# RG-LRU gate products from operands split into high and low parts, on TensorE

## The chip, the cores and the metric

One core of one Trainium2 chip. The metric is the device time of one execution of the whole kernel in microseconds (us). Every operand starts in device memory and the output ends there. The profile is of one execution; its times count from the start of the span, which runs from the first to the last recorded instruction.

## The reference

A trunk of two layers on x (1 x 512 x 1024, float32): one recurrent layer, one differential-attention layer that reads one shared K/V, each followed by a squared-ReLU MLP of width 4096. The change lies in the recurrent layer alone:

```
xy = rmsnorm(x) @ w_in + b_in            # 1024 -> 2048
xb, yb = split(xy);  gate = gelu(yb)
xc = causal_conv4(xb, conv_w) + conv_b   # per channel
g = einsum('bsnc,gncd->gbsnd', xc in 8 blocks of 128, gate_w) + gate_b
r = sigmoid(g[0]);  i = sigmoid(g[1])
log_a = -8 * r * softplus(-lam);  a = exp(log_a)
bx = sqrt(-expm1(2 * log_a)) * (i * xc)
hs = scan(h_t = a_t * h_(t-1) + bx_t)
out = (hs * gate) @ w_out
```

The gates' products are block-diagonal: for each of 8 blocks of 128 channels two products of a 128x128 weight with 128 x 512 values.

## The kernel before

Channels lie on the 128 partitions, the 512 positions in the free dimension; a chunk m is one block of 128 channels. Each engine runs a queue of its own in an order written out by hand, and counting semaphores join them: `wait_ge` holds an engine's queue until a semaphore has a value, so everything behind the waiting instruction waits too.

The large products are computed in three passes. A weight tile of 128 x 1024 (eight 128x128 blocks) is loaded by SP into `w_raw` (two buffers), ScalarE copies it to `w_hi` in the type float32r (`split_hi`, L630), VectorE subtracts to give `w_lo` (`split_lo`, L1167), and TensorE adds up w_hi x hi, w_hi x lo and w_lo x hi over the eight chunks: 24 matmuls of 128x128 by 128x512 (L1916). `w_hi` and `w_lo` have four slots, and a tile's PSUM bank is one of four, so tile t needs bank t-4 read. The load of tile r is issued when `split_lo` of tile r-2 is done; `split_hi(t)` waits for the load and for tile t-4 on TensorE.

The input product has 16 tiles, in the order x0 x1 x2 x3 x4 y0 x5 y1 x6 y2 x7 y3 y4 y5 y6 y7. VectorE evicts an x tile into `pad` (`branch`, L1289) and a y tile into `gelu` (`y_scaled`, L1295), scaled by `rstd`, which `norm_guess` on ScalarE and `norm_newton` on VectorE make just before the first eviction. For each chunk then: `tap` (ScalarE, L713) and `conv` (VectorE, three steps, L1301) give the convolution in `lru_v`; `gates(m)` (TensorE, L1975) makes the two gate products in two PSUM banks; `sigmoids` (ScalarE, L720 and L722), `gated_input` (VectorE, L1312), `tanh` (L729), `decay_exp` (L734), `decayed` (VectorE, L1318 and L1322), `root` (ScalarE, L739 and L741), `scaled_input` (L1328), `recurrence` (a scan, L1334), `gelu_of` (L746), `gated` (L1340), `gated_hi` (L751) and `gated_lo` (L1345) lead to the split operand of the output product. That starts with three tiles opened side by side, chunk by chunk (`open_tiles`), each step waiting for its chunk's `gated_lo`. Chunk m's gates stand in TensorE's queue behind input tile 4 (chunk 0), 5 (1 and 2), 6 (3), 7 (4), 9 (5), 10 (6) and 12 (7).

In `gates(m)` the weights `gw` and the moving operand `lru_v[:, m, :]` are plain float32, unsplit. `gw` is loaded by a DMA in ScalarE's queue (L699). ScalarE's functions belong to table sets; an ACT_TABLE_LOAD stands ahead of a function that the loaded set lacks (sigmoid and tanh share one, exp, sqrt and gelu need others; Copy and Identity never bring one).

Of the kernel before, what the change touches and what calls it, by code (L numbers as in the profile page):

```python
# [8 lines left out]
P = 128  # L9
D = 1024  # L10
S = 512
NCH = D // P
# [7 lines left out]
TILE = NCH * P  # L20
# [165 lines left out]
def build(nc, x_t, weights, gate_weights, vectors, lam_vecs, final_gain, out):  # L186
    F32 = mybir.dt.float32
# [5 lines left out]
    with keep:  # L193
        def sb(name, shape, dt, stack=keep):
            return stack.enter_context(nc.sbuf_tensor(name, shape, dt))

        def sem(name):
            return keep.enter_context(nc.semaphore(name))
# [11 lines left out]
        lru_v = sb("lru_v", [P, NCH, S], F32, region)  # L210
        lru_x = sb("lru_x", [P, NCH, S], F32, region)
        gelu = sb("gelu", [P, NCH, S], F32, region)
        sb("between", [P, 2, S], F32, region)
        early = ExitStack()
        gw = sb("gw", [P, 2 * NCH * P], F32, early)
        pad = sb("pad", [P, NCH, PAD + S], F32, early)
        early.close()
        out_hi = sb("out_hi", [P, NCH, S], F32R, region)
        out_lo = sb("out_lo", [P, NCH, S], F32R, region)
        region.close()  # L220
# [39 lines left out]
        results.close()  # L260
        prob = sb("prob", [P, 2, 2, S], F32)
        prob_t = sb("prob_t", [P, 2, S], F32)
        work = sb("work", [P, 4, S], F32)
        r21 = work[:, 0:2, :].rearrange("p n s -> p (n s)")
        a_sum = work[:, 2:4, :].rearrange("p n s -> p (n s)")
# [63 lines left out]
        conv_consts = sem("conv_consts")  # L329
        tap_done = sem("tap_done")  # L330
        conv_done = sem("conv_done")
        gates_mm = sem("gates_mm")
        gates_act = sem("gates_act")
        ix_done = sem("ix_done")
# [275 lines left out]
        def _(act):  # L610
            own = Own(act, act_own)
            def split_hi(t):
                if t >= TILES:
                    return
                quarter = quarter_of(t)
                if quarter is None:
                    r = RING_OF[t]
                    act.wait_ge(raw_in[r % RAWS], 16 * (r // RAWS))
                    src = w_raw[:, r % RAWS, :]
                else:  # L620
                    layer, g, (q, loaded, sums, adds), half = quarter
                    act.wait_ge(quarter_in[q][half], quarter_loads(layer, g, loaded))
                    if sums:
                        act.wait_ge(sum_in[q][half], quarter_sums(layer, g, q, sums))
                    if adds:
                        act.wait_ge(quarter_added, quarter_adds(layer, g, adds - 1, half))
                    src = QUARTERS[q][:, half, :]
                if t >= RING:
                    act.wait_ge(tile_done, t - RING + 1)
                nc.scalar.activation(w_hi[:, t % RING, :], src, ACT.Copy).then_inc(whi_done, 1)  # L630
# [26 lines left out]
            def norm_guess(n):  # L657

                act.wait_ge(stats_done, n + 1)
                k = n + (n > N_KV)  # L660
                by_cols, by_rows = cols[:, 1, :], work[:, 3, :]
                if n != N_A:
                    take_log(by_cols, ps[:, BANK_COLS, 0:QB], k)
                if n in (N_A, N_KV):
                    take_log(by_rows, ps[:, BANK_STATS, :], k + (n == N_KV))
                if n != N_A:
                    take_root(by_cols, k)
                if n in (N_A, N_KV):
                    take_root(by_rows, k + (n == N_KV))
# [40 lines left out]
            def tap(m):  # L710

                act.wait_ge(bank_read, XT[m] + 1)
                nc.scalar.activation(lru_v[:, m, :], pad[:, m, PAD:], ACT.Identity,  # L713
                                     scale=col("conv_w", PAD * NCH + m),
                                     bias=conv_c[:, m:m + 1]).then_inc(tap_done, 1)

            def sigmoids(m):
                act.wait_ge(gates_mm, m + 1)
                bank_r, bank_i = BANK_GATES[m % 2]
                nc.scalar.activation(lru_r[:, m, :], ps[:, bank_r, :], ACT.Sigmoid,  # L720
                                     bias=col("gate_b", m))
                nc.scalar.activation(lru_x[:, m, :], ps[:, bank_i, :], ACT.Sigmoid,  # L722
                                     bias=col("gate_b", NCH + m)).then_inc(gates_act, 1)

            def tanh(m):

                act.wait_ge(gates_act, m + 1)
                act.wait_ge(ix_done, m + 1)
                nc.scalar.activation(lru_v[:, m, :], lru_r[:, m, :], ACT.Tanh,  # L729
                                     scale=small[:, 8, m:m + 1]).then_inc(tanh_done, 1)  # L730

            def decay_exp(m):
                act.wait_ge(tanh_done, m + 1)
                nc.scalar.activation(lru_r[:, m, :], lru_r[:, m, :], ACT.Exp,  # L734
                                     scale=small[:, 9, m:m + 1]).then_inc(lru_exp, 1)

            def root(m):
                act.wait_ge(lru_q, m + 1)
                nc.scalar.activation(lru_v[:, m, :], lru_v[:, m, :], ACT.Sqrt,  # L739
                                     scale=-1.0).then_inc(sqrt_done, 1)  # L740
                nc.scalar.activation(lru_r[:, m, :], lru_r[:, m, :], ACT.Copy, scale=-1.0,  # L741
                                     bias=1.0).then_inc(lru_a, 1)
# [10 lines left out]
            act.wait_ge(consts_done, 1)  # L753
            split_hi(4)
            split_hi(5)
            norm_guess(N_A)
            act.wait_ge(conv_consts, 1)
            act.wait_ge(decay_done, 3)
            split_hi(6)
            tap(0)  # L760
            tap(1)
            tap(2)
            split_hi(7)
            split_hi(8)
            sigmoids(0)
            tap(3)
            tanh(0)
            tap(4)
            split_hi(9)
            sigmoids(1)  # L770
            sigmoids(2)
# [2 lines left out]
            tanh(2)  # L774
            split_hi(10)
            sigmoids(3)
            decay_exp(1)
            tap(5)
            decay_exp(2)
# [1 line left out]
            root(0)  # L781
            root(1)
            root(2)
            sigmoids(4)
            tanh(3)
            split_hi(12)
# [1 line left out]
            tanh(4)  # L788
            decay_exp(3)
            decay_exp(4)  # L790
            sigmoids(5)
            split_hi(13)
            split_hi(14)
# [1 line left out]
            sigmoids(6)  # L795
            tap(7)
            decay_exp(5)
            root(3)
            root(4)
            root(5)  # L800
# [353 lines left out]
        def _(dve):  # L1154
# [131 lines left out]
            def branch(m):  # L1286
                t = XT[m]
                dve.wait_ge(tile_done, t + 1)
                nc.vector.tensor_tensor(pad[:, m, PAD:], ps[:, t % RING, :], rstd[:, :],  # L1289
                                        ALU.mult).then_inc(bank_read, 1)  # L1290
# [7 lines left out]
            def conv(m):  # L1298
                dve.wait_ge(tap_done, m + 1)
                for j in range(PAD - 1, -1, -1):  # L1300
# [6 lines left out]
                    else:  # L1307
                        ins.then_inc(conv_done, 1)

            def gated_input(m):  # L1310
                dve.wait_ge(gates_act, m + 1)
                nc.vector.tensor_tensor(lru_x[:, m, :], lru_x[:, m, :], lru_v[:, m, :],  # L1312
                                        ALU.mult).then_inc(ix_done, 1)
# [12 lines left out]
            def scaled_input(c):  # L1326
                dve.wait_ge(sqrt_done, c + 1)
                own.step(nc.vector.tensor_tensor(lru_x[:, c, :], lru_x[:, c, :], lru_v[:, c, :],  # L1328
                                                 ALU.mult))
# [17 lines left out]

            split_lo(4)
            decay()
            norm_newton(N_A)  # L1350
            dve.wait_ge(conv_consts, 1)
            split_lo(5)
            branch(0)
# [2 lines left out]
            branch(2)  # L1356
            conv(0)
            branch(3)
            conv(1)
            split_lo(7)  # L1360
            branch(4)
            gated_input(0)
            conv(2)
            conv(3)
            gated_input(1)
            split_lo(8)
            y_scaled(0)
            gated_input(2)
            conv(4)
            branch(5)  # L1370
            split_lo(9)
            decayed(0)
            split_lo(10)
# [3 lines left out]
            y_scaled(1)  # L1377
            conv(5)
            scaled_input(0)
            recurrence(0)  # L1380
            split_lo(11)
            branch(6)
# [3 lines left out]
            split_lo(12)  # L1386
            conv(6)
            y_scaled(2)
            scaled_input(2)
            decayed(3)  # L1390
            gated_input(5)
# [3 lines left out]
            recurrence(2)  # L1395
            conv(7)
            decayed(5)
            gated_input(6)
            split_lo(14)
            y_scaled(3)  # L1400
# [508 lines left out]
        def _(pe):  # L1909
# [52 lines left out]
                ins.then_inc(stats_done, 1)  # L1962

            def gates(m):
                pe.wait_ge(conv_done, m + 1)
                if m == 0:
                    pe.wait_ge(gw_in, 16)
                if m == 1:

                    pe.wait_ge(rstd_done, N_A + 1)  # L1970
                if m >= 2:
                    pe.wait_ge(gates_act, m - 1)
                for g, bank in enumerate(BANK_GATES[m % 2]):
                    ws = slice((g * NCH + m) * P, (g * NCH + m + 1) * P)
                    ins = nc.tensor.matmul(ps[:, bank, :], gw[:, ws], lru_v[:, m, :], start=True, stop=True)  # L1975
                ins.then_inc(gates_mm, 1)

            pe.wait_ge(consts_done, 1)
# [424 lines left out]
```

## Time and profile before

| what | value |
|---|---|
| median of 3 runs | 1041.56 us (1040.28 to 1042.02) |
| the profiled execution | 1041.43 us |
| its span | 1038.9 us |
| mean granted TensorE clock | 0.997 |
| TensorE (PE) busy | 1022.2 us, 98% |
| VectorE (DVE) busy | 821.1 us, 79% |
| ScalarE (ACT) busy | 652.5 us, 63% |
| the 32 records of the gate products | between 37.4 and 95 us |

PE is TensorE's matmuls, PEld its weight loads, DVE VectorE, ACT ScalarE, POOL GpSimd, SP the queue that issues most loads. A float32 matmul shows as two records of the same instruction. A matmul's record is longer than the step from one start to the next, since matmuls are pipelined.

### The profile page before, as it was taken

How to read it: one execution, taken by the hardware profiler on the slowest of the kernel's cores; microseconds unless marked ns; L12 is line 12 of the kernel's file. 1: busy time of each engine (PE TensorE's matmuls, PEld its weight loads, DVE VectorE, ACT ScalarE, POOL GpSimd, SP SyncE). 2: the span in 40 equal slices, each digit the busy share in tenths (PEclk: the TensorE clock that was granted, in tenths of full speed). 3: DMA queues.
4: the chain of work that ended last, by engine and by line, in shares of the span. 5: the costliest groups of instructions: out<-in, count | busy, mean ns of one | idle time of the engine just before them, and what ended most of it. 6: DMA issues, size and time to landing. Idle time of an engine off the chain costs nothing.

```text
span 1038.9 us, 15457 instructions
## 1 busy us (share of the span) xinstructions
PE 1022.2 (98%) x5984; PEld 887.6 (85%) x5984; DVE 821.1 (79%) x1173; ACT 652.5 (63%) x956; POOL 107.7 (10%) x133
## 2 busy tenths in 40 slices
PE   8999999999999999999999999999999999999995
PEld 5777889989979989988888888879989989989984
DVE  7998886896896896898756877768697697697696
ACT  7698776745745755755436676757764664664665
POOL 1000110121111111010000000011021011011012
PEclk9999999999999999999999999999999999999998
DMA  7222856498498498472422111286498589589672
GB/s 254 87 92 65 227 142 185 114 255 231 113 244 239 118 241 242 121 182 82 122 61 62 62 62 62 89 229 131 160 206 222 180 198 231 179 185 229 194 171 93
DMA packets 47592, 165.29 MB, mean 159 GB/s; under 512 B 5408, under 2 KB 5536, under 8 KB 47392
## 3 DMA queue, kind: packets, MB, share of 16 engines
q1 hardware_dynamic: 31536, 109.59, 30.7%
q0 software_dynamic: 15552, 53.48, 28.5%
q10 hardware_dynamic: 432, 1.24, 0.3%
q8 instruction: 47, 0.77, 0.3%
q14 instruction: 25, 0.20, 0.1%
HBM read 159.05 MB, written 2.10 MB: 155 GB/s over the span
## 4 chain that ended last, share of the span: by engine, by line
PE 83%; DVE 7%; DMA 4%; issue 3%; ACT 2%; POOL 0%; SPq 0%; DVEq 0%; ACTq 0%; POOLq 0%
PE ps L2049 27%; PE ps L2084 24%; PE ps L1916 21%; PE ps L2147 4%; DVE w_lo L1167 3%; DMA w_raw<-weights 2%; PE ps L2211 2%; PE ps L2236 2%; PE ps L1975 1%; DMA q<-weights 1%; ACT w_hi L630 1%; PE ps L2225 1%; DVE r L1508 1%; DVE value L1546 1%; DMA x<-x_t 1%
## 5 line engine op out<-in xcount | busy, mean ns | idle before, releaser
L2049 PE MATMUL ps<-x_hi,w_hi 128*128 128x256 f32 x896 | 254.0, 284 | 0.2 <-DVE x_lo L1448 0.2
L2049 PE MATMUL ps<-x_hi,w_lo 128*128 128x256 f32 x896 | 253.6, 283 | 0.0
L2049 PE MATMUL ps<-x_lo,w_hi 128*128 128x256 f32 x896 | 253.5, 283 | 0.0
L630 ACT ACTIVATE w_hi<-w_raw 128x1024 fp32r<-128x1024 f32 x134 | 140.1, 1052 | 142.9 <-DMA w_raw<-weights 105.5
L1167 DVE TENSOR_TENSOR w_lo<-w_raw,w_hi 128x1024 fp32r<-128x1024 f32 x134 | 164.0, 1224 | 74.7 <-ACT w_hi L630 74.0
L1167 DVE TENSOR_TENSOR w_lo<-q,w_hi 128x1024 fp32r<-128x1024 f32 x144 | 176.5, 1229 | 48.6 <-ACT w_hi L630 47.8
L630 ACT ACTIVATE w_hi<-q 128x1024 fp32r<-128x1024 f32 x144 | 151.0, 1052 | 96.6 <-PE ps L2049 44.4
L2084 PE MATMUL ps<-w_hi,a_hi 128*128 128x512 f32 x448 | 176.3, 393 | 2.0 <-DVE w_lo L1167 1.2
L2084 PE MATMUL ps<-w_hi,a_lo 128*128 128x512 f32 x448 | 174.7, 390 | 0.0
L2084 PE MATMUL ps<-w_lo,a_hi 128*128 128x512 f32 x448 | 174.6, 390 | 0.0
L2049 PEld LDWEIGHTS ps<-x_hi,w_hi 128*128 128x128 f32 x896 | 171.9, 192 | 0.7 <-DVE x_lo L1448 0.4
L2049 PEld LDWEIGHTS ps<-x_lo,w_hi 128*128 128x128 f32 x896 | 172.0, 192 | 0.3
L2049 PEld LDWEIGHTS ps<-x_hi,w_lo 128*128 128x128 f32 x896 | 172.0, 192 | 0.0
L559 POOL DMA_DIRECT2D q<-weights x96 | 82.5, 941 | 836.3 <-DMA q<-weights 473.1
L2084 PEld LDWEIGHTS ps<-w_hi,a_hi 128*128 128x128 f32 x448 | 84.1, 188 | 26.0 <-issue 5.3
L2084 PEld LDWEIGHTS ps<-w_lo,a_hi 128*128 128x128 f32 x448 | 84.1, 188 | 17.8
L2084 PEld LDWEIGHTS ps<-w_hi,a_lo 128*128 128x128 f32 x448 | 84.2, 188 | 16.4
L1546 DVE SCALAR_TENSOR_TENSOR value<-ps,scale,value 128x512 f32<-128x512 f32 x104 | 73.1, 744 | 3.0 <-PE ps L2084 2.6
L1916 PE MATMUL ps<-in_hi,w_hi 128*128 128x512 f32 x128 | 53.6, 419 | 2.8 <-DVE in_lo L1172 1.4
L1916 PE MATMUL ps<-in_hi,w_lo 128*128 128x512 f32 x128 | 49.9, 390 | 0.0
L1916 PE MATMUL ps<-in_lo,w_hi 128*128 128x512 f32 x128 | 49.9, 390 | 0.0
L1535 DVE TENSOR_TENSOR a_lo<-work,a_hi 128x1024 fp32r<-128x1024 f32 x32 | 39.0, 1220 | 0.0
(226 smaller groups left out, 1670.3 us busy)
## 6 DMA issues: line engine op xcount, KB each, us to landing
w_raw<-weights SPq DMA_DIRECT2D x134, 512.0 KB, 4.2
q<-weights POOLq DMA_DIRECT2D x96, 512.0 KB, 7.9
q<-weights SPq DMA_DIRECT2D x64, 512.0 KB, 4.7
x<-x_t SPq DMA_DIRECT2D x8, 256.0 KB, 6.2
y_t<-value SPq DMA_DIRECT2D x8, 256.0 KB, 2.3
acc<-work POOLq DMA_DIRECT2D x6, 256.0 KB, 3.5
rstd<-work POOLq DMA_DIRECT2D x6, 256.0 KB, 3.3
w_raw<-weights SPq DMA_DIRECT2D x4, 256.0 KB, 4.6
```

The source lines that it names most:

```text
L559: nc.gpsimd.dma_start(QUARTERS[q][:, half, :], weights[stored_tile(layer, g, place + half)], accum_op=ALU.add).then_inc(sum_in[q][half], 16)
L630: nc.scalar.activation(w_hi[:, t % RING, :], src, ACT.Copy).then_inc(whi_done, 1)
L1167: nc.vector.tensor_tensor(w_lo[:, t % RING, :], src, w_hi[:, t % RING, :], ALU.subtract).then_inc(wlo_done, 1)
L1508: nc.vector.tensor_tensor(to[:, :], to[:, :], banks, ALU.add).then_inc(up_added, 1)
L1535: nc.vector.tensor_tensor(a_lo[:, k % SLOTS, :, :].rearrange("p n s -> p (n s)"), src, a_hi[:, k % SLOTS, :, :].rearrange("p n s -> p (n s)"),
L1546: return nc.vector.scalar_tensor_tensor(out=to, in0=bank, scalar=scale2[:, half, tok:tok + 1], in1=to, op0=ALU.mult, op1=ALU.add)
L1916: ins = nc.tensor.matmul(ps[:, bank, :], w[:, slot, ws], o[:, k, :], start=(k == 0 and n == 0), stop=(k == NCH - 1 and n == 2))
L2049: ins = nc.tensor.matmul(to, w[:, t % RING, ws], o[:, op, j, :], start=fresh and j == 0 and f % 2 == 0 and n == 0, stop=j == PAIRS - 1 and ...
L2084: ins = nc.tensor.matmul(ps[:, bank, :], a[:, a_slot, j, ts], w[:, slot, ws], start=first and a is a_hi and w is w_hi, stop=end and w is w ...
L2147: ins = nc.tensor.matmul(ps[:, 4 * half + tok, :], o[:, k, ts], w[:, t % RING, cs], start=(i == 0 and n == 0), stop=(i == NCH - 1 and n == 2))
L2211: ins = nc.tensor.matmul(ps[:, BANK_SCORES + 2 * (j % 2) + c, 0:n], q[rows, :], k[rows, :], start=i == 0, stop=i == 2)
L2236: ins = nc.tensor.matmul(ps[:, BANK_O, qb * P:(qb + 1) * P], prob_t[:, j % 2, kb * P:(kb + 1) * P], value[:, kb, h * P:(h + 1) * P], start ...
```

## The change

`gw` is split once into `gw_hi` (ScalarE, a float32r copy in two instructions of 128 x 1024) and `gw_lo` (VectorE, a subtract in two instructions, written over `gw`). For each chunk `conv_hi` (ScalarE) copies the convolution's result to `xc_hi` as float32r and `conv_lo` (VectorE) subtracts to give `xc_lo`; both have two buffers, so `conv_hi(m)` also waits for the products of chunk m-2. `gates(m)` makes six float32r matmuls of 128x128 by 128x512 in place of two float32 ones, and waits for `conv_lo(m)` in place of `conv(m)`. `between`, an unused spacer, moves behind the early tensors; `xc_hi` and `xc_lo` lie over `work`.

```diff
+            def gate_weights_hi(n):
+                ks = slice(n * TILE, (n + 1) * TILE)
+                act.wait_ge(gw_in, 16)
+                nc.scalar.activation(gw_hi[:, ks], gw[:, ks], ACT.Copy).then_inc(gw_hi_done, 1)
+            def conv_hi(m):
+                act.wait_ge(conv_done, m + 1)
+                if m >= 2:
+                    act.wait_ge(gates_mm, m - 1)
+                nc.scalar.activation(xc_hi[:, m % 2, :], lru_v[:, m, :], ACT.Copy).then_inc(xc_hi_done, 1)
...
+            def gate_weights_lo(n):
+                ks = slice(n * TILE, (n + 1) * TILE)
+                dve.wait_ge(gw_hi_done, n + 1)
+                nc.vector.tensor_tensor(gw_lo[:, ks], gw[:, ks], gw_hi[:, ks], ALU.subtract).then_inc(gw_lo_done, 1)
+            def conv_lo(m):
+                dve.wait_ge(xc_hi_done, m + 1)
+                nc.vector.tensor_tensor(xc_lo[:, m % 2, :], lru_v[:, m, :], xc_hi[:, m % 2, :],
+                                        ALU.subtract).then_inc(xc_lo_done, 1)
...
             def gates(m):
-                pe.wait_ge(conv_done, m + 1)
+                pe.wait_ge(xc_lo_done, m + 1)
                 if m == 0:
-                    pe.wait_ge(gw_in, 16)
+                    pe.wait_ge(gw_lo_done, 2)
...
-                    ins = nc.tensor.matmul(ps[:, bank, :], gw[:, ws], lru_v[:, m, :], start=True, stop=True)
+                    for i, (w, o) in enumerate(((gw_hi, xc_hi), (gw_hi, xc_lo), (gw_lo, xc_hi))):
+                        ins = nc.tensor.matmul(ps[:, bank, :], w[:, ws], o[:, m % 2, :], start=i == 0, stop=i == 2)
```

The queues of the changed kernel up to the last chunk, with what is added in capitals:

- ScalarE: split_hi(4), split_hi(5), GATE_WEIGHTS_HI(0), norm_guess, GATE_WEIGHTS_HI(1), split_hi(6), tap(0), tap(1), tap(2), CONV_HI(0), split_hi(7), CONV_HI(1), split_hi(8), sigmoids(0), tap(3), tanh(0), CONV_HI(2), tap(4), CONV_HI(3), split_hi(9), sigmoids(1), sigmoids(2), tanh(1), decay_exp(0), tanh(2), split_hi(10), sigmoids(3), CONV_HI(4), decay_exp(1), tap(5), decay_exp(2), split_hi(11), root(0), root(1), root(2), CONV_HI(5), sigmoids(4), tanh(3), split_hi(12), tap(6), tanh(4), decay_exp(3), decay_exp(4), CONV_HI(6), sigmoids(5), split_hi(13), split_hi(14), tanh(5), sigmoids(6), tap(7), decay_exp(5), CONV_HI(7), root(3), ...
- VectorE: split_lo(4), decay, GATE_WEIGHTS_LO(0), norm_newton, GATE_WEIGHTS_LO(1), split_lo(5), branch(0), split_lo(6), branch(1), branch(2), conv(0), branch(3), CONV_LO(0), conv(1), split_lo(7), CONV_LO(1), branch(4), gated_input(0), conv(2), conv(3), CONV_LO(2), CONV_LO(3), gated_input(1), split_lo(8), y_scaled(0), gated_input(2), conv(4), branch(5), CONV_LO(4), split_lo(9), decayed(0), split_lo(10), gated_input(3), decayed(1), decayed(2), y_scaled(1), conv(5), scaled_input(0), CONV_LO(5), recurrence(0), split_lo(11), branch(6), scaled_input(1), recurrence(1), gated_input(4), split_lo(12), conv(6), y_scaled(2), CONV_LO(6), scaled_input(2), decayed(3), gated_input(5), branch(7), decayed(4), split_lo(13), recurrence(2), conv(7), decayed(5), CONV_LO(7), gated_input(6), ...

## Rows read from the trace of the kernel before

**Rows 1.** The page, busy time, share of the span and instructions.
```profile
PE 1022.2 (98%) x5984; PEld 887.6 (85%) x5984; DVE 821.1 (79%) x1173; ACT 652.5 (63%) x956; POOL 107.7 (10%) x133
```

**Rows 2.** The chain that ended last: start us, us, what.
```profile
29.85 1.23 DVE w_lo L1167
...
31.82 5.72 PE ps L1916 x24
37.55 1.72 PE ps L1975 x4
...
95.06 59.89 PE ps L1916 x264
```

**Rows 3.** TensorE's waits, 28 to 125 us: in total, times, longest.
```profile
PE ps L1916 <- DVE pad L1289: 0.4, 1, 0.4
```

**Rows 4.** TensorE's time line: start us, us, line, instruction, idle time before.
```profile
1.65 3.78 PE L1981 MATMUL ps<-three_halves,ones 128*128 128x512 f32 x4 [1.65 <-POOL cols L520]
...
37.16 0.39 PE L1916 MATMUL ps<-in_hi,w_lo 128*128 128x512 f32 x1
37.39 1.88 PE L1975 MATMUL ps<-lru_v,gw 128*128 128x512 f32 x4
...
39.33 0.40 PE L1916 MATMUL ps<-in_lo,w_hi 128*128 128x512 f32 x1
...
1029.09 0.39 PE L2084 MATMUL ps<-w_lo,a_hi 128*128 128x512 f32 x1
```

**Rows 5.** VectorE's time line, the same columns.
```profile
29.85 1.23 DVE L1167 TENSOR_TENSOR w_lo<-w_raw,w_hi 128x1024 fp32r<-128x1024 f32 x1
30.99 0.68 DVE L1289 TENSOR_TENSOR pad<-ps,rstd 128x512 f32<-128x512 f32 x1
...
33.92 2.32 DVE L1301 SCALAR_TENSOR_TENSOR lru_v<-pad,vec,lru_v 128x512 f32<-128x512 f32 x3
36.16 0.68 DVE L1289 TENSOR_TENSOR pad<-ps,rstd 128x512 f32<-128x512 f32 x1
...
55.42 0.69 DVE L1318 SCALAR_TENSOR_TENSOR lru_r<-lru_r,lru_v 128x512 f32<-128x512 f32 x1
...
56.75 1.22 DVE L1167 TENSOR_TENSOR w_lo<-w_raw,w_hi 128x1024 fp32r<-128x1024 f32 x1
...
65.73 1.22 DVE L1334 TENSOR_TENSOR_SCAN lru_v<-lru_r,lru_x 128x512 f32<-128x512 f32 x1
```

**Rows 6.** ScalarE's time line, the same columns.
```profile
38.72 1.28 ACT L720 ACT_TABLE_LOAD   x1
40.01 0.69 ACT L720 ACTIVATE lru_r<-ps,vec 128x512 f32<-128x512 f32 x1
40.60 0.68 ACT L722 ACTIVATE lru_x<-ps,vec 128x512 f32<-128x512 f32 x1
41.17 0.81 ACT L713 ACTIVATE lru_v<-pad,conv_c,vec 128x512 f32<-128x512 f32 x1
...
97.69 1.06 ACT L630 ACTIVATE w_hi<-w_raw 128x1024 fp32r<-128x1024 f32 x1
...
103.64 0.73 ACT L734 ACTIVATE lru_r<-lru_r,small 128x512 f32<-128x512 f32 x1
104.27 0.62 ACT L751 ACTIVATE out_hi<-lru_v 128x512 fp32r<-128x512 f32 x1
```

**Rows 7.** The ring's loads issued between 30 and 60 us.
```profile
DMA to landing us min/median/max: 3.3/3.5/4.4
```

**Rows 8.** The gate weights' load, its issue (first and last start).
```profile
L699 ACTq DMA_DIRECT2D gw<-gate_weights x1: 335/335/335, 12.8 to 12.8; - x1
```

**Rows 9.** A window near the end: busy by engine, granted clock, DMA share, GB/s.
```profile
1033.00:1033.50 0.50, 0.00 (x0) 0.00 (x0) 0.02 (x1) 0.45 (x1) 0.00 (x0) 0.67 0.50 188
```

**Rows 10.** VectorE's waits, 30 to 125 us: in total, times, longest.
```profile
DVE pad L1289 <- PE ps L1916: 3.3, 2, 2.7
DVE lru_x L1312 <- ACT lru_x L722: 2.0, 3, 1.3
...
```

More of the change, by code:

```diff
@@ L212, in build @@
         gelu = sb("gelu", [P, NCH, S], F32, region)
-        sb("between", [P, 2, S], F32, region)
+        early = ExitStack()
+        gw_lo = sb("gw_lo", [P, 2 * NCH * P], F32R, early)
+        early.close()
         early = ExitStack()
         gw = sb("gw", [P, 2 * NCH * P], F32, early)
+        gw_hi = sb("gw_hi", [P, 2 * NCH * P], F32R, early)
         pad = sb("pad", [P, NCH, PAD + S], F32, early)
         early.close()
+        sb("between", [P, 2, S], F32, region)
         out_hi = sb("out_hi", [P, NCH, S], F32R, region)
@@ L262, in build @@
         prob_t = sb("prob_t", [P, 2, S], F32)
+        early = ExitStack()
+        xc_hi = sb("xc_hi", [P, 2, S], F32R, early)
+        xc_lo = sb("xc_lo", [P, 2, S], F32R, early)
+        early.close()
         work = sb("work", [P, 4, S], F32)
@@ L331, in build @@
         conv_done = sem("conv_done")
+        gw_hi_done = sem("gw_hi_done")
+        gw_lo_done = sem("gw_lo_done")
+        xc_hi_done = sem("xc_hi_done")
+        xc_lo_done = sem("xc_lo_done")
         gates_mm = sem("gates_mm")
@@ L755, in _ @@
             split_hi(5)
+            gate_weights_hi(0)
             norm_guess(N_A)
+            gate_weights_hi(1)
             act.wait_ge(conv_consts, 1)
@@ L762, in _ @@
             tap(2)
+            conv_hi(0)
             split_hi(7)
+            conv_hi(1)
             split_hi(8)
@@ L767, in _ @@
             tanh(0)
+            conv_hi(2)
             tap(4)
+            conv_hi(3)
             split_hi(9)
@@ L776, in _ @@
             sigmoids(3)
+            conv_hi(4)
             decay_exp(1)
@@ L783, in _ @@
             root(2)
+            conv_hi(5)
             sigmoids(4)
@@ L790, in _ @@
             decay_exp(4)
+            conv_hi(6)
             sigmoids(5)
@@ L797, in _ @@
             decay_exp(5)
+            conv_hi(7)
             root(3)
@@ L1349, in _ @@
             decay()
+            gate_weights_lo(0)
             norm_newton(N_A)
+            gate_weights_lo(1)
             dve.wait_ge(conv_consts, 1)
@@ L1358, in _ @@
             branch(3)
+            conv_lo(0)
             conv(1)
             split_lo(7)
+            conv_lo(1)
             branch(4)
@@ L1364, in _ @@
             conv(3)
+            conv_lo(2)
+            conv_lo(3)
             gated_input(1)
@@ L1370, in _ @@
             branch(5)
+            conv_lo(4)
             split_lo(9)
@@ L1379, in _ @@
             scaled_input(0)
+            conv_lo(5)
             recurrence(0)
@@ L1388, in _ @@
             y_scaled(2)
+            conv_lo(6)
             scaled_input(2)
@@ L1397, in _ @@
             decayed(5)
+            conv_lo(7)
             gated_input(6)
```

## The prediction

> **What bounds the kernel now.** I read the page first: TensorE is busy for 98% of the span [rows 1]. Then the chain that ended last: from 95.06 us it runs 59.89 us through TensorE alone, and around the gates it is TensorE too, tile of weights by tile of weights, with 1.72 us for each pair of gate products [rows 2]. Just ahead of that it is VectorE's: a w_lo subtract at 29.85, then the first eviction, and TensorE's tile 4 starts at 31.82 [rows 2], 0.4 us late, the only wait TensorE has between 28 and 125 us [rows 3]. So what TensorE loses or saves in this stage arrives at the end unchanged, and what VectorE is given before 31.8 is paid in full. Elsewhere in the stage VectorE and ScalarE work for nearly all of the time, in hand-written orders, and the question is whether their new work still comes before TensorE asks for it. My working is the trace's time line carried on, queue by queue.
>
> **TensorE's saving.** A gate pair is two unsplit 128x512 products, shown as four records. The last tile matmul starts at 37.16, the second one after the pair at 39.33; less two ordinary steps of 0.227 (the steps ahead of 37.39 in the row; a tile of 24 takes 5.45) the pair costs 2.17 - 0.45 = 1.72 us [rows 4]. The new six products have the shape and types of the tile's own: 6 x 0.227 = 1.36 us. Eight pairs save 8 x 0.36 = 2.9 us. Each restart after a wait costs 0.08 (0.31 instead of 0.23), the only dearer bound.
> The page "FP8 and Floating Point Precision", section TensorE Precision Notes, of the Trainium skill says that a true FP32 product takes four passes through the array. By that the pair would be eight passes against six, a quarter saved, 0.43 us of 1.72 and 3.4 us over the eight; the trace's six single steps leave less, and the sum goes by the trace.
>
> **Prices on the two feeders.** Instructions that wait for nothing start 0.08 to 0.1 us before the end of the one ahead (w_lo 29.85 + 1.23, next at 30.99 [rows 5]), so each counts with its duration less 0.09. VectorE: 1.14 for a 1024-wide subtract or a scan, 0.60 for a 512-wide one, 2.24 for a convolution, 1.33 for decayed() [rows 5]. ScalarE: 0.97 for 1024 wide, 0.52 for a 512-wide Copy, 0.59 and 0.58 for the sigmoids, 0.7 for a tap, 0.63 for tanh or exp, and 1.28 for each table load, which starts as soon as the queue reaches it, even before its operand is there [rows 6]. The in-place subtract gw_lo over gw has no twin in this stage; I price it as the row of its shape. A ring load is issued when w_lo two tiles earlier is done, and lands 3.5 us later (3.3 to 4.4) [rows 7]. gw itself is issued at 12.8 [rows 8], ten us before it is now first read, so its load costs nothing. The added ScalarE and VectorE work is 2 x 0.97 + 8 x 0.52 = 6.1 us and 2 x 1.14 + 8 x 0.60 = 7.1 us.
>
> **Before tile 4.** gate_weights_hi(0) and (1) sit in ScalarE's idle time and end at 25.3 and 27.6, hidden. gate_weights_lo(0), after decay(), and gate_weights_lo(1), before split_lo(5), are both on the chain to branch(0): 2 x 1.14 = 2.28 us. branch(0) ends at 33.95, tile 4 starts at 34.10 in place of 31.82. **+2.28.**
>
> **gates(0).** conv(0) ends at 38.52 (36.24 + 2.28). conv_hi(0) ends 39.17, conv_lo(0) 39.89, so gates(0) can start at 40.04; tile 4 gives TensorE free at 39.67. **+0.45** with the restart. It ends at 41.5, and tile 5 fills TensorE to 46.9.
>
> **gates(2), the large one.** VectorE goes on with conv(1) 39.80 to 42.12. ScalarE has conv_hi(1) queued behind that wait: 42.16 to 42.78. Behind it stand split_hi(8) (to 43.7), and only then the table load for sigmoids(0) (43.74 to 45.02) and the two sigmoids, to 46.30; before, they were done at 41.28 [rows 6]. VectorE's gated_input(0) waits for them, until 46.33, and behind it are conv(2), from 46.93 to 49.25, and conv(3), to 51.49. conv_lo(2) stands behind conv(3): 51.40 to 52.09. TensorE, after gates(1) (46.93 to 48.29), needs xc_lo(2) and gets it at 52.24. Before, it ran gates 1 and 2 without a gap. **+3.95 + 0.08.** gates(1) itself is covered (conv_lo(1) ends 43.87). After gates(2) TensorE stands at 53.7, 5.7 us later than before.
>
> **What is late next.** conv_hi(3) waits for conv(3) and ends at 52.15; split_hi(9), sigmoids(1) and (2) follow to 55.45; gated_input(1) is let go at 54.3; split_lo(8) ends only at 56.14 and so the load of tile 10 lands at 59.9. ScalarE's split_hi(10) waits for it (TensorE frees the ring slot at 59.4 anyway), then come a table load, sigmoids(3) and conv_hi(4), 63.46 to 64.08. VectorE is through with branch(5) at 60.09 and stands in conv_lo(4) for 4.0 us, to 64.12; the result is there at 64.81, before TensorE ends tile 7 at 65.94: gates(3) and (4) cost no wait. But split_lo(9) now ends at 65.94, the load of tile 11 lands at 69.7 and holds ScalarE at split_hi(11); roots 0 to 2 run to 75.3, conv_hi(5) to 75.9, conv_lo(5) to 76.6, against gates(5) asked for at 78.2: covered by 1.5 us. Then ScalarE: sigmoids(4) to 78.5, tanh(3), split_hi(12), tap(6) to 80.8. VectorE: recurrence(0), split_lo(11), branch(6), scaled_input(1), recurrence(1), gated_input(4), split_lo(12) from 76.5 to 83.1, conv(6) to 85.39, y_scaled(2). conv_hi(6) ends at 86.05, conv_lo(6) at 86.77, and TensorE has finished tile 10 at 85.01: gates(6) at 86.92. **+1.91 + 0.08.** gates(7) is asked for at 99.3 and its operand is ready at 97.7: covered.
>
> **The output product.** TensorE reaches the three open tiles at 117.0 (before 111.3). Each step of three k chunks lasts 2.04. ScalarE and VectorE are later by about 8.5 us than before there: gated_lo(0) ends at 115.1, in time; gated_lo(1) stands behind split_lo(18), which waits for gelu(3), gelu(4) and split_hi(18), and ends at 119.57, while TensorE asks at 118.33: **+1.39.** Behind it chunks 2 to 7 come 0.1 to 3 us before they are asked for (the last at 131.2, asked for at 132.0). Everything behind lies as before, shifted: TensorE is the chain again.
>
> **Sum.** 2.28 + 0.45 + 4.03 + 1.99 + 1.39 - 2.9 = +7.2 us. The profiled execution took 1041.43 us (span 1038.9 and 2.5 around it), the median of the runs is 1041.56; I take 1041.4 + 7.2 = **1048.6 us**. The least certain terms are the last two, 3.4 us together, since they are differences of long queues: a table load or a DMA of 1 us more or less moves them fully. 0.2% of the time, 2.1 us, is about what can be told from no change.
>
> **Rivals.**
> The late stalls don't come. VectorE has 4 us of idle time in my line at conv_lo(4), and if ScalarE's queue is 2 us faster than I make it, gates(6) and the output product are covered. Then 2.28 + 0.45 + 4.03 - 2.9 = +3.9: 1045.3 us. Against it: both engines' waits in my line come from a load and a ring slot, which no faster arithmetic moves.
> The clock falls in the wait at gates(2). Before, the granted clock was still 1.00 until 1033.0 and 0.67 in the next half microsecond, on the way to 0.50 [rows 9], 3.7 us after the last matmul, started at 1029.09, had ended [rows 4]; my wait is 3.8 to 3.9 us, at the edge. At the low clock the four warm-up records took 3.78 us where the four gate records take 1.88 [rows 4], and at 6.36 the pace was full: 1.9 to 2.4 us lost. As gates(6) is held by VectorE and not by TensorE, up to 2.0 of it is swallowed there: 1048.6 to 1049.0; if the wait at gates(6) isn't there for other reasons, or gates(2) comes later still, up to 1051. The page "TensorE: Matmul & The Clock Gate" of the Trainium skill, section HAM oscillation, has the rule that a pause in TensorE's work halves its clock and each restart then begins slowly; the fall at 1033 agrees.
> It comes out faster, or the same. If ScalarE reached sigmoids(0) before conv_hi(1)'s wait mattered, or conv_lo(2) were ready by 48.3, the one stall of 4.03 would be gone and with it the later two, and 2.28 + 0.45 - 2.9 = -0.2 remains: 1041.2. To be faster by 2.1 us, the 2.28 ahead of tile 4 must be hidden too, -2.9: 1038.5. It decides at stalls of 2.9 us in all. Against it: the order of VectorE alone (conv(2), conv(3), conv_lo(2) behind gated_input(0)) puts 5.8 us between the end of sigmoids(0) and xc_lo(2), while TensorE has one tile and one pair.
> Two engines' added work might also cost its whole 7.1 us on top of my waits, were there no idle time to take it up; VectorE waited for 9.0 us between 30 and 125, the sum of six rows of which the two largest are shown [rows 10], and could take it up; so I give that little, 1052 us and more.
>
> **Chances.** My line, with its neighbours 1046.3 to 1050: 0.62. Late stalls gone, 1044 to 1046.3: 0.15. Clock or further waits, 1050 and over: 0.13. Stalls absent, no change: 0.05; faster by over 0.2%: 0.05. The range 1044 to 1051.8 leaves out these last two and some 5 in 100 above. Faster 0.05, same 0.05, slower 0.90.
>
> **What would show it.** In the profile of the changed kernel: TensorE waiting 2.3 us more ahead of tile 4, for the pad eviction; six matmuls of 0.39 at a step of 0.23 in place of four of 0.59; a wait of about 4 us for xc_lo near 48 us, the largest of the stage; another of about 2 us near 85; one of over 1 us for out_lo near 118; VectorE idle for 4 us near 60, let go by xc_hi; sigmoids(0) ending near 46.3. The forecast falls if xc_lo(2) is ready by 48, which needs sigmoids(0) some 4 us sooner, or if TensorE later waits for something now hidden from it, so that the delay is taken up there.

## The result, and the profile after

The changed kernel takes 1051.22 us in the median (1051.01 to 1052.82, 4 runs), the kernel before 1040.92 on the same occasion: a ratio of 1.0103, 95% interval 1.0091 to 1.0115. It is 10.3 us slower. The forecast was 1048.6, slower by 7.2, with a range of 1044.0 to 1051.8: the direction and the range held, the difference was 3.1 us larger than forecast. Two later sets of executions of the same two kernels put it at 9.5 and 8.9 us, so it is 1.7 to 3.1 us above the forecast's 7.2. The profiled execution of the changed kernel took 1051.01 us; its span is 1048.5 and its mean granted clock 0.992.

TensorE's waits of the changed kernel, 28 to 125 us, the same view as [rows 3]:

```profile
PE ps L2031 <- DVE xc_lo L1352: 3.4, 2, 2.6
PE ps L1971 <- DVE pad L1324: 2.1, 1, 2.1
PE ps L1971 <- DVE out_lo L1390: 1.2, 1, 1.2
```

Where there was one wait of 0.4 us there are four, and they are the ones that were named: ahead of tile 4, twice for xc_lo, once for out_lo. TensorE's time line shows where, and what the passes cost now (compare [rows 4]):

```profile
33.35 0.47 PE L1971 MATMUL ps<-in_hi,w_hi 128*128 128x512 f32 x1 [2.07 <-DVE pad L1324]
...
51.45 0.50 PE L2031 MATMUL ps<-xc_hi,gw_hi 128*128 128x512 f32 x1 [2.61 <-DVE xc_lo L1352]
...
66.80 0.39 PE L2031 MATMUL ps<-xc_hi,gw_hi 128*128 128x512 f32 x1
67.03 0.39 PE L2031 MATMUL ps<-xc_lo,gw_hi 128*128 128x512 f32 x1
...
68.16 0.39 PE L1971 MATMUL ps<-in_hi,w_hi 128*128 128x512 f32 x1
...
86.80 0.50 PE L2031 MATMUL ps<-xc_hi,gw_hi 128*128 128x512 f32 x1 [0.80 <-DVE xc_lo L1352]
...
119.55 0.50 PE L1971 MATMUL ps<-out_hi,w_hi 128*128 128x512 f32 x1 [1.18 <-DVE out_lo L1390]
```

Six passes from 66.80 to 68.16 are 1.36 us, to the digit. The bracket is idle time counted from the modelled end of the record ahead, 0.16 us (0.39 less a step of 0.23) after TensorE could have issued the next; so 2.07 there is 2.23 by the prediction's way of counting.

The stage's end is best read from one line, VectorE's eviction of the output product, which is the same instruction in both kernels. Durations min/median/max, then first and last start; before, and after:

```profile
L1455 DVE TENSOR_TENSOR x<-x,ps x8: 678/680/689, 125.8 to 155.0; 128x512 f32<-128x512 f32 x8
```

```profile
L1510 DVE TENSOR_TENSOR x<-x,ps x8: 679/680/689, 132.8 to 162.1; 128x512 f32<-128x512 f32 x8
```

The last start moves from 155.0 to 162.1: 7.1 us in the stage, where 7.2 were forecast. The span grew by 9.6. So 2.5 us of this execution went behind the stage, where the forecast had nothing.

What it had as a rival only is the clock. Windows of the changed kernel (busy by engine, granted clock, DMA share, GB/s):

```profile
34.00:35.00 1.00, 1.00 (x6) 0.78 (x5) 1.00 (x3) 0.09 (x2) 0.00 (x0) 0.87 0.76 303
35.00:36.00 1.00, 1.00 (x4) 0.81 (x3) 1.00 (x2) 1.00 (x2) 0.00 (x0) 0.50 1.01 234
38.00:39.00 1.00, 1.00 (x6) 0.81 (x5) 0.90 (x2) 1.00 (x2) 0.00 (x0) 0.92 0.01 4
51.00:52.00 1.00, 0.55 (x2) 0.51 (x3) 0.90 (x2) 1.00 (x2) 0.00 (x0) 0.91 0.03 8
53.00:54.00 1.00, 1.00 (x4) 0.79 (x3) 0.41 (x1) 0.56 (x1) 0.00 (x0) 0.50 0.00 0
55.00:56.00 1.00, 1.00 (x5) 0.77 (x5) 1.00 (x3) 1.00 (x2) 0.00 (x0) 0.89 0.00 0
727.00:728.00 1.00, 0.83 (x6) 0.74 (x7) 0.89 (x1) 1.00 (x4) 0.62 (x1) 0.83 0.80 307
729.00:730.00 1.00, 1.00 (x6) 1.00 (x5) 0.97 (x1) 0.91 (x1) 0.49 (x1) 0.50 0.76 164
731.00:732.00 1.00, 1.00 (x10) 1.00 (x9) 0.76 (x1) 0.97 (x5) 0.00 (x0) 0.97 1.07 197
```

Three times the clock is at its lower level (0.50 of full, 1.2 GHz). A window at 0.87 spent 0.26 us low, one at 0.92 spent 0.16, and the three between them all of it: 3.4 us, during which TensorE does half its work (a tile's matmuls step by 0.43 us there, in place of 0.23) and so loses 1.7. The first fall comes 1.4 us after tile 4 has started, the second 0.4 after gates(2) has, and the third near 728 us, in the second layer, where the only wait just ahead is of 0.17 us, as in the kernel before. In the profile of the kernel before the clock was full until the last matmuls were done.

### The profile page after: what moved, and what is told of

It reads as the page before. It is cut to its first block, busy times and chain, and to the rows that moved or that the text cites. A ratio compares the mean times of both kernels' runs of the same rounds, so it can differ in the third digit from the quotient of the medians.

```text
span 1048.5 us, 15516 instructions
## 1 busy us (share of the span) xinstructions
PE 1026.2 (98%) x6000; PEld 895.9 (85%) x6000; DVE 828.4 (79%) x1183; ACT 659.3 (63%) x966; POOL 107.5 (10%) x133
## 4 chain that ended last, share of the span: by engine, by line
PE 66%; DVE 13%; ACT 7%; issue 7%; DMA 7%; POOL 0%; SPq 0%; DVEq 0%; ACTq 0%; POOLq 0%
PE ps L2105 23%; PE ps L2140 17%; PE ps L1971 15%; DVE w_lo L1202 5%; PE ps L2203 4%; DMA w_raw<-weights 4%; ACT w_hi L643 3%; DMA q<-weights 2%; PE ps L2267 2%; PE ps L2292 2%; DVE r L1563 1%; DVE value L1601 1%; DVE lru_v L1336 1%; PE ps L2281 1%; DVE work L1572 1%
```

## The experiments

Each is told with its median beside that of the kernel before on the same chip and, where it decides, the last start of the output product's eviction in its profile (155.0 before, 162.1 after). The part ahead of the first eviction, branch(0), differs by up to 1 us between executions of one kernel, so some stretches are counted from the start of branch(0) to that last start: 124.0 us before (155.0 - 30.99), 129.6 after (162.1 - 32.53).

**The passes alone.** The kernel before, with only the products changed:

```diff
-                    ins = nc.tensor.matmul(ps[:, bank, :], gw[:, ws], lru_v[:, m, :], start=True, stop=True)
+                    for i in range(3):
+                        ins = nc.tensor.matmul(ps[:, bank, :], in_hi[:, m, :P], in_hi[:, m, :], start=i == 0, stop=i == 2)
```

> The kernel before, with six float32r matmuls per chunk in place of the two float32 ones, on operands that lie ready (in_hi for weights and values); no split is added and no wait is changed, and the gates' values are left out. If the passes are worth what one tile step says, 8 x 0.36 = 2.9 us go: about 1038. If the float32 pair were hidden behind something else, or the switch between types cost as much, the time stays at 1041.

1039.1 us (1036.81 to 1041.11, 10 runs) beside 1041.54; ratio 0.9979, 0.9966 to 0.9991. The eviction of its output product:

```profile
L1455 DVE TENSOR_TENSOR x<-x,ps x8: 679/682/689, 122.4 to 151.7; 128x512 f32<-128x512 f32 x8
```

The last eviction starts 3.3 us sooner (3.2 counted from branch(0)), the median is 2.4 us lower. The saving is real, and a little larger than 2.9: from the start of gates(0) to the start of gates(1), one pair and one tile, it is 7.20 us before and 6.80 here, 0.40 for a pair in place of 0.36.

**Without the weights' low part.** The changed kernel, third pass with gw_hi:

```diff
-            gate_weights_lo(0)
-            gate_weights_lo(1)
-                    pe.wait_ge(gw_lo_done, 2)
+                    pe.wait_ge(gw_hi_done, 2)
-                    for i, (w, o) in enumerate(((gw_hi, xc_hi), (gw_hi, xc_lo), (gw_lo, xc_hi))):
+                    for i, (w, o) in enumerate(((gw_hi, xc_hi), (gw_hi, xc_lo), (gw_hi, xc_hi))):
```

> The changed kernel without the two subtracts that make gw_lo (the third pass uses gw_hi, so the low part of the weights is left out). My account: they are on the chain to tile 4, so tile 4 starts 2.3 us earlier, the clock does not fall there, and ScalarE's and VectorE's whole line moves up by as much: about 1048.8, and 1.7 less if the fall near 728 us goes too. Rival: the stage is held by the splits of the convolution alone, and the 2.3 us are taken up at gates(2): 1051.

1049.28 us (1048.02 to 1052.04, 4 runs) beside 1041.54; ratio 1.0086, 1.0063 to 1.0109. TensorE's time line, where it waits:

```profile
31.75 0.47 PE L1969 MATMUL ps<-in_hi,w_hi 128*128 128x512 f32 x1 [0.41 <-DVE pad L1324]
...
49.85 0.50 PE L2029 MATMUL ps<-xc_hi,gw_hi 128*128 128x512 f32 x1 [3.78 <-DVE xc_lo L1352]
```

The wait ahead of tile 4 is back at 0.41, the clock doesn't fall there, and the wait at gates(2) is 3.78 us, with the 0.16 of the modelled record the forecast's 3.95. The stage ends at 160.4, 1.7 us sooner than in the first profile of the changed kernel, where 2.3 were expected, and 1.1 to 2.9 us sooner than in its three profiles. Counted from branch(0) it takes 129.5 us, as before the edit (129.6), so what went is what stood ahead of branch(0). That shows the two subtracts on the path. The times alone don't: the ratios 1.0086 here and 1.0084 to 1.0103 for the changed kernel overlap, so the time of the rival, 1051, is not ruled out by them.

**gates(2) behind tile 6.**

```diff
-            gates_after = {4: (0,), 5: (1, 2), 6: (3,), 7: (4,), 9: (5,), 10: (6,), 12: (7,)}
+            gates_after = {4: (0,), 5: (1,), 6: (2, 3), 7: (4,), 9: (5,), 10: (6,), 12: (7,)}
```

> The changed kernel with gates(2) behind input tile 6 in place of tile 5 in TensorE's queue. The 2.6 us wait before gates(2) should go, as tile 6 fills it. My account: the end of the stage is set by ScalarE's and VectorE's line and not by TensorE, so what is won here is given back at gates(6) and at the output product: 1050 to 1051.5. Rival: TensorE's waits simply add, and the 2.6 us and 1.7 us of low clock drop out: about 1047.

1050.83 us (1048.39 to 1053.39, 4 runs) beside 1041.54; ratio 1.0098, 1.0073 to 1.0122. The waits for xc_lo only move, from before gates(2) to before gates(4):

```profile
65.94 0.77 PE L2031 MATMUL ps<-xc_hi,gw_hi 128*128 128x512 f32 x1 [2.83 <-DVE xc_lo L1352]
87.63 0.50 PE L2031 MATMUL ps<-xc_hi,gw_hi 128*128 128x512 f32 x1 [0.77 <-DVE xc_lo L1352]
```

The stage ends at 162.9, 129.7 us after branch(0) began. To fill a wait of TensorE with TensorE's own next work wins nothing while its feeders are what is late.

**The splits without the passes.** The changed kernel's feeders, with TensorE as before:

```diff
-                nc.vector.tensor_tensor(gw_lo[:, ks], gw[:, ks], gw_hi[:, ks], ALU.subtract).then_inc(gw_lo_done, 1)
+                nc.vector.tensor_tensor(gw_hi[:, ks], gw[:, ks], gw_hi[:, ks], ALU.subtract).then_inc(gw_lo_done, 1)
-                pe.wait_ge(xc_lo_done, m + 1)
+                pe.wait_ge(conv_done, m + 1)
-                    pe.wait_ge(gw_lo_done, 2)
+                    pe.wait_ge(gw_in, 16)
-                    for i, (w, o) in enumerate(((gw_hi, xc_hi), (gw_hi, xc_lo), (gw_lo, xc_hi))):
-                        ins = nc.tensor.matmul(ps[:, bank, :], w[:, ws], o[:, m % 2, :], start=i == 0, stop=i == 2)
+                    ins = nc.tensor.matmul(ps[:, bank, :], gw[:, ws], lru_v[:, m, :], start=True, stop=True)
```

> The changed kernel with its splits in place on ScalarE and VectorE, in the same queues, but TensorE makes the two float32 products of before and waits for the convolution only; the second subtract of the weights writes over gw_hi so that gw stays whole. My account: the feeders' line is as late as in the changed kernel and holds the output product, so about 1050 to 1051, although TensorE waits for no split. Rival: the waits for xc_lo make the loss, and without them the time is the 2.3 us ahead of tile 4 and little else: 1043.5 to 1045.

1049.48 us (1047.41 to 1051.82, 4 runs) beside 1041.54; ratio 1.0085, 1.0061 to 1.0109. TensorE's waits, and the eviction:

```profile
PE ps L1971 <- DVE pad L1324: 2.7, 1, 2.7
PE ps L2030 <- DVE lru_v L1336: 2.2, 2, 1.6
PE ps L1971 <- DVE out_lo L1390: 1.8, 1, 1.8
```

```profile
L1510 DVE TENSOR_TENSOR x<-x,ps x8: 679/681/689, 133.0 to 162.2; 128x512 f32<-128x512 f32 x8
```

TensorE waits for no split and has 2.9 us more to compute, and the stage ends at 162.2, within 0.1 us of the changed kernel. Counted from branch(0) it takes 128.9 us, against 128.3 to 129.7 in three profiles of the changed kernel, and TensorE still waits 1.8 us for out_lo. So the end of the stage is set by ScalarE's and VectorE's queues, and not by what TensorE computes. In this profile the clock never fell before the last matmuls, although the wait ahead of tile 4 is 2.7 us, longer than the one of 2.1 behind which it fell in the changed kernel. It is the fastest of the four executions, 1047.41 us with a mean granted clock of 0.997; the other three, at 0.993 and 0.994, will have had falls.

**Does the late loss come from the moment?** The kernel before, with idle products ahead of the output product (eight, or four):

```diff
+            pe.wait_ge(gates_act, NCH)
+            for _ in range(8):
+                nc.tensor.matmul(ps[:, BANK_STATS, :], ones[:, :], rstd[:, :], start=True, stop=True)
             open_tiles(T_OUT, OPEN, out_hi, out_lo, O_Y, lag=1)
```

> The kernel before, nothing of the change, with eight idle float32 products (128x512, into a free bank) ahead of the output product: TensorE runs on at its pace, and everything behind comes about 6.9 us later, nearly as late as in the changed kernel (7.1). My account of what the changed kernel loses behind the recurrent stage (2.5 us, 1.7 of it a fall of the clock near 728 us): it comes from the moment at which the later stages begin, not from the change's own work. Then this run shows a fall near 728 too and takes 1048 + 1.7 = about 1050. Rival: the loss belongs to the change, and this takes 1048.4.

> The same with four idle products, 3.4 us later: by the arithmetic of the products alone 1045.0. If the clock's fall in the second layer depends on the moment, it may be there or not, 1.7 us more or none; if it comes from any delay at all, it is there as in the run with eight.

With eight: 1047.98 us (1046.42 to 1048.99, 4 runs) beside 1040.8; ratio 1.0068, 1.0049 to 1.0087; its last eviction starts at 161.8. With four: 1045.77 (1043.3 to 1047.45, 7 runs); ratio 1.0045, 1.003 to 1.006; 158.2. Neither profile has the fall near 728 us. Here my account fell: a kernel that comes as late into the later stages doesn't lose more there. The one with eight costs what its products cost (7.2 us, 6.9 expected), and the changed kernel 1.7 to 3.1 us more (8.9 to 10.3). The one with four costs 5.0 us, 1.6 more than its products; the interval reaches down to 3.1, so that is no clear difference.

**The same work in another order.** Same instructions. ScalarE's queue now begins

```
split_hi(4), split_hi(5), norm_guess(N_A), gate_weights_hi(0), tap(0), tap(1), split_hi(6), gate_weights_hi(1),
conv_hi(0), conv_hi(1), split_hi(7), tap(2), tap(3), sigmoids(0), conv_hi(2), sigmoids(1), split_hi(8),
conv_hi(3), split_hi(9), tap(4), tanh(0), tanh(1), sigmoids(2), sigmoids(3), ...
```

and VectorE's

```
split_lo(4), decay(), norm_newton(N_A), branch(0), branch(1), branch(2), split_lo(5), conv(0), conv(1),
gate_weights_lo(0), gate_weights_lo(1), split_lo(6), conv_lo(0), conv_lo(1), branch(3), split_lo(7), conv(2),
conv(3), gated_input(0), conv_lo(2), gated_input(1), branch(4), conv_lo(3), ...
```

```diff
-            gates_after = {4: (0,), 5: (1, 2), 6: (3,), 7: (4,), 9: (5,), 10: (6,), 12: (7,)}
+            gates_after = {5: (0, 1), 6: (2, 3), 8: (4,), 10: (5, 6), 13: (7,)}
```

> The changed kernel with the same instructions, in another order on ScalarE and VectorE, and the gates behind tiles 5 (0 and 1), 6 (2 and 3), 8 (4), 10 (5 and 6) and 13 (7): the weights' subtracts come after the first evictions, sigmoids are not queued behind a convolution that is still running, and so on. My account: the order makes the loss, not the amount of work, so TensorE waits for nothing in the stage, and 2.9 us of the passes and the 0.4 ahead of tile 4 are won: the last eviction of the output product 3.3 us earlier than before, about 1038. Rival: the 6.1 us more on ScalarE and 7.1 us more on VectorE don't fit beside TensorE in any order, and the time stays above 1043.

1038.12 us (1035.9 to 1040.7, 12 runs) beside 1040.8 (20 runs); ratio 0.9973, 0.9962 to 0.9983: faster than both kernels. Its profile has no wait of TensorE between 28 and 125 us. Its eviction of the output product:

```profile
L1510 DVE TENSOR_TENSOR x<-x,ps x8: 676/680/689, 121.7 to 151.0; 128x512 f32<-128x512 f32 x8
```

The window from 30 to 125 us (busy PE, PEld, DVE, ACT, POOL), of this kernel and then of the changed one:

```profile
30.00:125.00 95.00, 95.00 (x421) 78.64 (x420) 92.16 (x126) 84.66 (x114) 3.60 (x4) 1.00 0.39 116
```

```profile
30.00:125.00 95.00, 88.34 (x372) 71.48 (x371) 83.68 (x113) 78.30 (x103) 0.98 (x1) 0.96 0.29 92
```

VectorE is busy for 92.2 of 95 us, and still TensorE never waits. The last eviction starts at 151.0, 4.0 us ahead of the kernel before (3.3 expected). The work fits; in the order of the changed kernel it did not. The new order differs in many places of three queues at once, so it shows that the order makes the loss, and not which of its steps makes how much: no run moves conv_hi(1) or conv_lo(2) alone.

**TensorE kept busy in its two long waits.** The changed kernel, with idle products:

```diff
+            def idle(bank, n):
+                for _ in range(n):
+                    nc.tensor.matmul(ps[:, bank, :], ones[:, :], three_halves[:, :], start=True, stop=True)
             def gates(m):
+                if m == 2:
+                    pe.wait_ge(gates_act, 1)
+                    idle(4, 4)
...
+                if t == 4:
+                    pe.wait_ge(rstd_done, N_A + 1)
+                    idle(7, 2)
                 tile_starts(t, t - RING + 1)
```

> The changed kernel, with TensorE kept busy in its two longest waits of the stage: two idle float32 products ahead of tile 4 and four ahead of gates(2), into banks that are free. The two early falls of the clock should go. My account: the 1.7 us that each cost TensorE were taken up by the waits that follow, because ScalarE's and VectorE's line sets the end of the stage, so the last eviction of the output product stays within 0.5 us of the changed kernel's. On the later fall near 728 us: each of the three profiles that had it also had an early fall, and none of the four without an early fall had it; if the one brings the other, it is gone here, and the time is 1049.3; if not, 1051. Rival for the stage: the early falls cost their 3.4 us, and the output product ends by 3 us sooner.

> The changed kernel once more, unaltered, on the same chip as the run that keeps TensorE busy: 1051, with the clock's falls near 35, 52 and 728 us if they belong to the kernel, and without some of them if they differ from one execution to the next.

Kept busy: 1048.0 us (1047.13 to 1049.32, 4 runs), ratio 1.0066, 1.0051 to 1.0082. Unaltered: 1050.99 (1049.14 to 1052.45, 4 runs), ratio 1.0095, 1.0073 to 1.0116; before 1041.52. Both were repeated, with more executions:

> The same kernel that keeps TensorE busy in its waits, in more rounds, beside the unaltered one. Both profiles so far ended the output product within 1.1 us of each other, but the medians differed by 3. If the early falls cost nothing, as I hold from the stage, the medians come within 1.5 us of each other and the profile's last eviction is again near that of the changed kernel. Rival: low clock early is worth about 3 us in most executions, and the medians differ by that again.

> The changed kernel unaltered, beside the last one: 1050 to 1051, with the early falls near 35 and 52 us again. If the early falls cost nothing, within 1.5 us of the other; by the rival 3 us more.

Kept busy: 1048.28 us (1045.91 to 1049.51, 5 runs), ratio 1.0051, 1.0034 to 1.0068. Unaltered: 1050.81 (1050.2 to 1052.39, 5 runs), ratio 1.0084, 1.0068 to 1.0099; before 1041.87. Twice the medians differ by 2.5 to 3.0 us, so the expectation that they come within 1.5 us fell, and the rival's 3 us stands. (The profiles without an early fall were six by then, not four as the expectation has it: those of the kernel before, the passes alone, the splits without the passes, eight and four idle products, and the new order; none has the fall near 728.)

Of three profiles of the changed kernel all have the fall near 35 us, two the one near 52, and two the one near 728. Of the two with TensorE kept busy none has an early fall, and one has the late one:

```profile
729.00:730.00 1.00, 1.00 (x6) 1.00 (x6) 0.68 (x1) 1.00 (x2) 0.00 (x0) 0.50 0.96 184
```

So the early falls don't bring the late one, and the late one differs from one execution of the same kernel to the next. What the fall near 52 costs shows on ScalarE, at split_hi(10), which needs tile 6 done and its load landed; first the changed kernel's first profile, then the one whose clock didn't fall at gates(2):

```profile
60.26 1.06 ACT L643 ACTIVATE w_hi<-w_raw 128x1024 fp32r<-128x1024 f32 x1 [1.61 <-PE ps L1971]
```

```profile
59.71 1.06 ACT L643 ACTIVATE w_hi<-w_raw 128x1024 fp32r<-128x1024 f32 x1 [1.08 <-DMA w_raw<-weights]
```

Counted from the start of branch(0), at 32.53 and 33.18, it is 27.7 against 26.5 us: tile 6 at half pace was later than the load. From branch(0) to the last eviction the changed kernel takes 129.6, 129.7 and 128.3 us in its three profiles (162.1 - 32.53, 163.3 - 33.56, 161.5 - 33.18), the third the one without that fall; kept busy it takes 128.8 and 128.9 (162.2 - 33.41, 161.7 - 32.77); before, 124.0.

## Why the prediction was right, and where it fell short

**What bounds.** Right. The stage's 7.1 us come through to the end, and 2.5 us are added behind it. The measured 1051.2 lies in the band of 1050 and over, "clock or further waits", which had a chance of 0.13, and not in that of the main line (0.62): the way and the mechanism were forecast, and the size was held by the range.

**The passes, -2.9.** Right: 1.36 us for six steps, and 3.2 to 3.3 us in the stage when made alone. In the changed kernel none of it reaches the end, since TensorE isn't what is late: with the passes the stage ends at 162.1, without at 162.2. The sum hid this, as it took 2.9 off and made each later wait larger by as much; the total is the same.

**Ahead of tile 4, +2.28.** The mechanism is right. The time line shows 33.35 in place of 31.82, 1.53 later, because the early part of this execution ran 0.7 us sooner: the w_lo subtract ahead of the weights' subtracts starts at 21.92, and at 22.66 before. Over all profiles branch(0) starts at 33.1 us in the mean in the seven with these subtracts ahead of it, and at 30.9 in the five without: 2.2 later.

**gates(0), +0.45.** Hidden in the changed kernel, since tile 4, at the low clock, took 7.2 us in place of 5.45. Where the clock stayed full it is there: without the weights' low part, and with TensorE kept busy, gates(0) and what follows it come 0.41 us late.

**gates(2), +4.03.** Place and cause are right: conv_lo(2) behind conv(3), behind gated_input(0), behind sigmoids(0), behind a conv_hi(1) that waits. The wait is 2.6 us because TensorE came to it 1.7 us late, having run at the low clock from 34.7 to 38.2; where that fall was absent it was 3.8.

**What is late next.** Right in every place, though not in every size: VectorE idle until xc_hi(4) for 3.6 us (4.0), the wait at gates(6) with TensorE going on at 86.80 (86.92), and the wait for out_lo(1) with TensorE going on at 119.55 (118.33 + 1.39 = 119.72). Three of VectorE's lines:

```profile
64.45 0.69 DVE L1352 TENSOR_TENSOR xc_lo<-lru_v,xc_hi 128x512 fp32r<-128x512 f32 x1 [3.56 <-ACT xc_hi L740]
...
75.93 0.69 DVE L1352 TENSOR_TENSOR xc_lo<-lru_v,xc_hi 128x512 fp32r<-128x512 f32 x1 [0.50 <-ACT xc_hi L740]
...
130.57 0.69 DVE L1390 TENSOR_TENSOR out_lo<-lru_v,out_hi 128x512 fp32r<-128x512 f32 x1 [0.70 <-ACT out_hi L776]
```

The prediction's line had these at 64.1, 75.9 and, as an end at 131.2, 130.5. The wait at gates(6) is 1.0 us (0.80, and 0.24 for the modelled end and the restart) where the sum has 1.99, since TensorE came there late through the second fall; with TensorE kept busy it is 1.60 and 1.74, near to it.

**The total.** On TensorE's time line the stage's loss adds up as 1.5 ahead of tile 4, 1.7 of low clock in tile 4, 2.9 at gates(2), 1.7 of low clock behind it, 1.0 at gates(6) and 1.4 at the output product, less 3.2 for the passes: 7.0. The forecast's 7.2 has other terms, and that the two meet so closely is in part luck. The early part came 0.7 us sooner than it might, and the clock made the stage behind branch(0) 5.6 us longer where the forecast has 5.0. The last evictions of the changed kernel's three profiles lie 6.5, 7.1 and 8.3 us behind that of the kernel before.

**The clock, the term that was mis-sized.** The prediction kept it for a rival at gates(2) alone, with up to 2.0 of its 1.9 to 2.4 us swallowed at gates(6). The 1.9 is from the pace of the four warm-up records, where the granted clock is shown as 1.00; a fall measured 1.7. It fell in two places, ahead of which TensorE had waited 2.1 and 2.6 us, for 1.7 us of TensorE's time each. The first was swallowed by the wait at gates(2). The second was not swallowed whole: through split_hi(10), which waits for tile 6, some 0.8 to 1.3 us went into the feeders' line (129.6 and 129.7 against 128.8, 128.9 and 128.3). And the late fall was in no account. With TensorE kept busy the same kernel takes 1048.0 and 1048.3 us, near the forecast's 1048.6; the 2.5 to 3.0 us above that are what the idle products take away. The section HAM oscillation of the page "TensorE: Matmul & The Clock Gate" of the Trainium skill says that a wait of TensorE can drop its clock each time it comes, and that each drop has its own cost. The falls behind the waits at 33 and 51 us agree; the one near 728 us, with no more than 0.17 us of wait just ahead, is not of this kind.

**What stays open.** Of those 2.5 to 3.0 us the profiles place 0.8 or so in the stage (129.6 and 129.7 against 128.8 and 128.9), and in the third profile none. The rest lies behind the stage. From the last eviction to the end of the span, the six profiles of all runs that have a late fall (near 728 us, or once near 1001 and once near 1011) take 885.2 to 887.5 us, and the seven that have none 882.8 to 885.3, 2.7 us less in the mean. Three of the six also waited for 1.9 to 2.0 us between 1000 and 1012 us; the other three take 885.2 to 887.0. So the 2.5 us between the changed kernel's first profile (886.4) and that of the kernel before (883.9) are about what goes with a late fall. The fall near 728 us is in five of the eight profiles that have the splits in their first order and in none of the five others, which is suggestive and no more; neither the moment nor the early falls explain it.

Each execution's mean granted clock says more than the few profiles. A fall of 3.4 us takes 0.0016 off it. It is 0.9929 in the mean of the 13 executions of the changed kernel in these sets, 0.9967 in the 9 with TensorE kept busy, and 0.9963 in 49 of the kernel before. By this estimate the changed kernel has 2.3 falls more per execution than with TensorE kept busy. Five early falls in three profiles are 1.7 per execution, so some 0.6 of a fall is left for the later stages, or 1 us. With the 0.8 us in the stage that leaves about 1 us of the 2.5 to 3.0 without a place.

## What to carry to other kernels

A split of an operand costs little busy time; what decides is where its two instructions stand in in-order queues. Here, in the trace, a Copy of 0.6 us that waited for a convolution held back two sigmoids, and through them VectorE and TensorE; and the same instructions in another order throughout turned 9 to 10 us lost into 2.7 us won. And where the bound engine pauses, look at its clock behind the pause, and at who waits for the slower work, before calling the loss hidden.

## What the runs showed of the hardware

In the changed kernel's first profile the clock fell behind waits of 2.1 and 2.6 us, after work had begun again, and stayed low for 3.4 us with TensorE busy; in its third it fell at 33.7, 0.3 us before the end of the wait ahead of tile 4. At the end of the kernel before it stayed full for 3.7 us after the last matmul [rows 4, 9]. So in some executions a pause shorter than that was enough. In others it was not: there was no fall behind the 2.7 us ahead of tile 4 with the splits alone, nor behind this wait at gates(2) in the changed kernel's third profile:

```profile
52.11 0.50 PE L2031 MATMUL ps<-xc_hi,gw_hi 128*128 128x512 f32 x1 [2.77 <-DVE xc_lo L1352]
```

So the length of a wait alone doesn't tell whether the clock falls. The kernel with the passes alone had one fall, at 1000.7 us, 0.5 us after its longest wait:

```profile
1000.20 0.47 PE L2085 MATMUL ps<-w_hi,a_hi 128*128 128x512 f32 x1 [1.89 <-DVE value L1546]
```

The kernel before waited 0.28 us at this place, and the changed kernel's third profile 2.0, without a fall there; so waits of the later stages differ between executions, too. Runs of one kernel on one chip lay up to 5 us apart (1038.62 to 1043.73 for the kernel before, 20 runs), so that four runs of a kernel would hardly have shown 2.7 us; here twelve stand beside twenty.
